# Paged sample NSA: where the transposes of a pair's probabilities and its value products stand in the order of units

## The reference, cut to what matters

```python
past = cache_nsa_paged[l][page_table].reshape(b_s, past_len, 4, NSA_KV_HEADS, HEAD_DIM)
rows = jnp.concatenate([past, new_rows], axis=1)
ctx = nsa_context(rows[:, :, 0], rows[:, :, 1], rows[:, :, 2], rows[:, :, 3], cmp_w)

def compress_kv(k, pe, w1, w2):          # keys and values, blocks of 32 with stride 16
    ...
    return jax.nn.gelu(flat @ w1) @ w2

# nsa_attend
s = jnp.einsum('bqgrd,bcgd->bgrqc', qc, k_cmp) * scale
p_cmp, _ = masked_softmax(s, cmp_end[None, :] <= q_pos[:, None])
o_cmp = jnp.einsum('bgrqc,bcgd->bqgrd', p_cmp.astype(v_cmp.dtype), v_cmp)
imp = jnp.einsum('bgrqc,cn->bgqn', p_cmp, cover)
top_val, top_idx = lax.top_k(score, SEL_TOPN)
...
p_sel, _ = masked_softmax(s, ...)        # over the selected blocks
o_sel = jnp.einsum('bgrqk,bgqkd->bqgrd', p_sel.astype(vs.dtype), vs...)
```

## Time and profile before

| what | value |
|---|---|
| median of 3 runs | 1140.96 us |
| lowest, highest run | 1134.28, 1141.26 us |
| the profiled execution | 1134.21 us |
| its span in the profile | 1132.3 us |
| its mean granted TensorE clock | 0.958 of 2.4 GHz |

### The profile page before, as it was taken

How to read it: one execution, slowest core, us unless ns; L and a number is a source line. 1 busy time by engine, 2 the same in 40 slices (tenths; PEclk the granted TensorE clock), 3 DMA queues, 4 the chain that set the end, 5 groups by cost and what they waited for, 6 DMA issues and landing times. The chain is left out here.

```text
span 1132.3 us, 20636 instructions
## 1 busy us (share of the span) xinstructions
PE 1037.0 (92%) x8408; PEld 775.5 (68%) x8408; DVE 476.9 (42%) x985; ACT 311.5 (28%) x678; POOL 148.1 (13%) x188
## 2 busy tenths in 40 slices
PE   6999999999889998888999999999998999788685
PEld 6999999899857677766987878776555433233232
DVE  6443433324267755544575747535126111110105
ACT  4100000221146644323555554511111111110103
POOL 0270000600015520000110000000001121101200
PEclk9999999999969999898999999999998999898988
DMA  8667871679355746784555333339907999999966
GB/s 258 243 224 290 298 252 27 198 270 321 111 188 187 261 150 188 246 275 187 203 187 207 149 150 149 117 113 334 381 19 282 376 425 424 424 422 425 424 256 249
DMA packets 100367, 279.92 MB, mean 247 GB/s; under 512 B 17764, under 2 KB 73984, under 8 KB 88896
## 3 DMA queue, kind: packets, MB, share of 16 engines
q1 hardware_dynamic: 90240, 229.57, 55.2%
q0 software_dynamic: 6976, 42.48, 9.8%
q10 hardware_dynamic: 3072, 6.75, 1.6%
HBM read 264.52 MB, written 69.53 MB: 295 GB/s over the span
## 5 line engine op out<-in xcount | busy, mean ns | idle before, releaser
L3128 PE MATMUL ex_up_ps<-ex_w_up,ex_hT 128*64 128x512 f32 x512 | 123.3, 637 | 26.6 <-DMA ex_w_up<-in_expert_w_up 25.0
L125 PE MATMUL proj_acc<-w_in_upper,hT_upper 128*128 128x328 f32 x352 | 112.3, 319 | 2.4 <-DVE hT_rest L119 2.1
L127 PE MATMUL proj_acc<-w_in_upper,hT_rest 128*128 128x328 f32 x352 | 110.5, 314 | 0.0
L3128 PEld LDWEIGHTS ex_up_ps<-ex_w_up,ex_hT 128*64 128x64 f32 x512 | 41.2, 146 | 97.3 <-issue 86.2
L126 PE MATMUL proj_acc<-w_in_rest,hT_upper 128*128 128x328 f32 x252 | 79.8, 317 | 0.0
L125 PE MATMUL sn_hp<-sn_xT,cmp_w_upper 128*128 128x256 f32 x256 | 76.4, 299 | 0.0
L125 PE MATMUL proj_acc<-hT_upper,merge_w_upper 128*128 128x272 f32 x256 | 74.3, 290 | 1.3 <-ACT qT_dil L564 1.3
L126 PE MATMUL proj_acc<-hT_rest,merge_w_upper 128*128 128x272 f32 x256 | 73.6, 288 | 0.0
L127 PE MATMUL proj_acc<-hT_upper,merge_w_rest 128*128 128x272 f32 x256 | 73.5, 287 | 0.0
L126 PE MATMUL sn_hp<-sn_xT,cmp_w_upper 128*128 128x256 f32 x256 | 73.2, 286 | 0.0
L127 PE MATMUL sn_hp<-sn_xT,cmp_w_rest 128*128 128x256 f32 x256 | 73.0, 285 | 0.0
(11 more groups left out here) (535 smaller groups left out, 1992.9 us busy)
## 6 DMA issues: line engine op xcount, KB each, us to landing
ex_w_up<-in_expert_w_up SPq DMA_DIRECT2D x30, 2048.0 KB, 30.9
ex_w_down<-in_expert_w_down SPq DMA_DIRECT2D x32, 1024.0 KB, 35.1
out_dil_sample<-in_cache_dil_w SPq DMA_DIRECT2D x16, 1022.0 KB, 9.1
out_dil_sample<-in_cache_dil_w SPq DMA_DIRECT2D x4, 4088.0 KB, 16.1
w_in_chunk<-in_w_in SPq DMA_DIRECT2D x10, 1312.0 KB, 6.0
merge_w<-in_w_in SPq DMA_DIRECT2D x16, 512.0 KB, 6.8
sd_kv_g<-in_cache_dil_w SPq DMA_DIRECT2D x16, 512.0 KB, 8.3
rows<-in_cache_dil_w SPq DMA_DIRECT2D x16, 512.0 KB, 7.5
```

What stands on the lines that cost most here:

```text
L125: pe.matmul(out, a[0], b[0], start=first, stop=False)
L127: return pe.matmul(out, a[1], b[0], start=False, stop=last)
L3128: ins = pe.matmul(up_ps[r, q, :], hT[:, q, c, r], wu[slot][:, u, c, :], start=c == 0, stop=c == KD - 1)
```

## The change

The units "p" and "c" of pair p stood behind the last unit of sequence 2p + 3. For pairs 0 and 1 they now stand behind the first unit (k0) of sequence 2p + 4. For pairs 2 and 3 nothing moves. No instruction is added or removed; the turns of `sn_misc` follow the list, so that `compressed` of sequence 3 (and 5) now comes ahead of `values` of pair 0 (and 1).

```diff
             for j, (kind, h) in enumerate(order):
                 add(kind, n, h, j)
-            if n % 2 == 1 and n > 1:
-                add("p", n // 2 - 1, 0)
-                add("c", n // 2 - 1, 0)
-        add("p", PAIRS - 1, 0)
-        add("c", PAIRS - 1, 0)
+                if j == 0 and n % 2 == 0 and n >= 4:
+                    add("p", n // 2 - 2, 0)
+                    add("c", n // 2 - 2, 0)
+        for p in (PAIRS - 2, PAIRS - 1):
+            add("p", p, 0)
+            add("c", p, 0)
```

## The result

| | kernel before | changed |
|---|---|---|
| median of 11 runs each | 1134.28 us | 1128.11 us |
| lowest, highest | 1131.33, 1141.26 | 1125.68, 1135.80 |
| profiled execution | 1134.21 | 1129.81 |
| span | 1132.3 | 1127.9 |

The ratio is 0.9939, with a 95% interval of 0.9919 to 0.9959: 6.9 us less, between 4.6 and 9.2. The forecast was 1136.8 with 1129 as the low end. The direction is right, the time lies 0.9 us under the range, and the gain is larger than the 4.2 us that the sum gave. The two medians lie 6.2 us apart, inside this interval.

What follows compares the result with a forecast made beforehand. TensorE was taken to set the pace up to slice 30, expert weights behind it. The exponential's 2.76 us and the arranging's 1.43 us sum to 4.2 us, so 1141.0 - 4.2 = 1136.8 us, range 1129 to 1142.

Steps and rivals of the forecast that it cites:

- What bounds the kernel: TensorE sets the pace up to slice 30, expert weights behind it; time given back in the sample stage reaches the end.
- Wait 1: TensorE's wait for ScalarE's exponential ahead of the probabilities' transposes, pairs 0 and 1: gone, 2 x 1.38 = 2.76 us.
- wait 2: TensorE's wait for VectorE's arranging ahead of v0's transposes, pairs 0 and 1: gone, 0.72 + 0.71 = 1.43 us.
- The work itself: At the boundary, no instruction added or removed; TensorE's rows are the same in another order, cost nil.
- Wait 3: Wait at the bank `sn_misc`, 0.24 us, stays; counted 0, bounds 0.24 gained or 0.3 lost for each pair.
- The clock weighed apart: Behind pair 1's exponential wait the granted clock falls to 0.51, costing 1.50 us; kept out of the sum as a rival.
- (a): Rival: the clock drop behind pair 1's wait goes too, 4.2 + 1.5 = 5.7 us, 1135.3 us; chance 0.20.
- The anchor: The whole kernel's starting time: shown median 1140.96 us of runs 1134.28, 1140.96 and 1141.26, less 4.2 us.
- (b): Rival: a wait moves to "c"'s small transposes or k0's transposes; half the gain returns, 2.1 us, 1138.9 us; chance 0.10.
- (c): Rival: the gain is swallowed by the expert weights at the end, 1141.0 us; chance 0.05.
- (d): Rival: gather 8 (12 for pair 1) lands late, k0's arranging holds TensorE; slower, 1145.4 us; chance 0.03.
- The chances: For the whole kernel: forecast time 0.60; over 1% faster 0.05, over 1% slower 0.02, within 1% 0.93.

Runs made afterwards that it cites:

- each edit alone: Kernel before with ScalarE's exponential ahead of the copy of the values: 1131.65 us; kernel before with v0's arranging right behind k0's: 1134.27 us.
- both waits treated in the old order: Kernel before, old unit order, with the exponential ahead of the copy of the values and v0's arranging right behind k0's: 1131.33 us, ratio 0.9953.

## Why the prediction was right and wrong

**What bounds the kernel, and that a gain in the stage reaches the end: right.** The quiet slice stayed and the rest of the program is as long as before.

**Wait 1 and wait 2 are gone: right** in place and number of waits, and each edit alone takes away its own, the exponential's down to 0.30 us. The term was 2 x 1.38 + 1.43 = 4.19 us, summed from brackets. Measured from start to start the first costs 1.53 us each and the second 0.67, 4.4 us for both pairs: 0.2 more, a small error of size.

**The work itself: a step that failed.** "TensorE's rows at the boundary are the same in another order, so their cost is nil" put the order at nothing. The runs show that the same sets of transposes take less time in the new places: 0.5 us at each boundary, 1.0 us for both. With both waits treated in the old order, 0.94 us at pair 0 still separated it from the changed kernel, and 0.48 of it is this.

**Wait 3 stays: right**, 0.25 and 0.29 us at `scores_compressed`, counted as 0.

**The clock weighed apart: the other step that failed.** "The trace bears it out for one wait of two, so I keep it out of the sum" put the forecast on a kernel before without a drop, and took 1.5 us out of the likeliest case. Half a drop for each wait was what the trace of before showed, and it is what the traces since have shown (4 of 9 places with a wait of 1.37 or 1.38 us). The mean saving of about 1 us belonged in the sum. In time alone the clock's part can't be told from noise.

**Why the time fell outside the range.** The low end, 1129, was built from the lower level of the runs, 1134.2 less 4.2 to 5.7, and the kernel before, timed beside the changed one, had just that median, 1134.28. So the level did not put the time outside; the gain did, since the order and the clock were not in it. With 5.4 for the boundaries and 1.0 for the clock, 1134.3 gives 1127.9, beside 1128.11 measured. Even rival (a) at the lower level, 1128.6, would have been 0.5 us too long.

**The anchor: what put the single figure 8.7 us too high.** "From the median: 1141.0 - 4.2" took the median of three runs as the kernel's time. Over 30 runs the kernel before has 1135.4, and 1139 us and above is reached in 6 of the 30. Two of the three shown were such runs. The working named two levels and then took the upper one for its forecast. This is 6 to 7 us of the miss; the other 2.2 us are the terms above.

**The rivals.** (a), the drop goes too, is right for these two traces: before had the drop at pair 1 and the changed kernel none. Its 5.7 us is close to the 6.4 of the traces partly by luck, since it counts a full drop and leaves out the order. (b) holds in a mild form: the chain that was named as the thinnest has 0.5 us, and an added 1.05 us shows there at once. (c) didn't occur. (d) didn't: the gather had landed, and k0 was arranged 1.1 us ahead of need. **The chances**: within 1% had 0.93, and 0.61% it is.

In the result 4 of the 11 runs of before stand at 1139 us and above, and none of the changed kernel's (highest 1135.80), so such runs may have grown rarer; that the drops in this stage make them isn't shown, and one drop of 1.5 us is too small for it.

What stays open is in which stage the runs of about 1140 us lose the clock, why one wait of 1.4 us is followed by a drop and another is not, and why a set of transposes takes 0.8 us in one place and 1.1 in another.

## What to carry to other kernels

Read what a wait costs on TensorE from start to start of the work around it, against the same stretch with that wait alone taken away: here the brackets of 1.37 and 0.72 us were worth 1.53 and 0.67, and a drop of the clock that may follow costs as much again as the longer wait, or twice that. The same work in another order isn't free of cost or gain; compare the starts of its groups too. When a unit is moved away from what it waited for, look for the next thinnest chain (here the casts behind the exponential, 0.5 us) and for the turn that comes too soon when it is moved once more. Take no median of three runs as an anchor when they fall at two levels.

## What the runs showed of the hardware

The granted clock fell to half at idle times as short as 1.37 us (7 of 13 places with 1.37 to 2.46 us at the boundaries). It stayed there for 3.4 us in five cases, which cost some 1.5 us of a dense stretch, and for 6.8 us in two, which cost 2.8 us in the one that can be read alone. At boundaries with 0.72 us or less it never fell (0 of 13). Two sets of eight transposes took 2.14 us when they stood behind each other and ahead of the value products, and 0.79 + 0.87 = 1.66 us when they stood ahead of a unit's products and ahead of s0's transposes, with no wait in either case.
